# One block of the program instead of two in a retention, short-convolution and product-key expert step

## The reference, cut to what matters

```python
mod = silu(c) @ W_ada + b_ada            # 6 parts: shift, scale, gate, twice
h = rms_norm(x, g_pre1) * (1 + scale1) + shift1
q, k, v, g, bg, cg, xv = split(h @ W_in) # 7 groups of 512 columns
m = concat(retention(q, k, v, g), short_conv(bg, cg, xv)) @ W_out
x = x + gate1 * rms_norm(m, g_post1)
h = rms_norm(x, g_pre2) * (1 + scale2) + shift2
# experts: 128 * 128 of them, 8 heads, 16 chosen in each head
s = (h @ W_q) . sub_keys                 # 16 score sets of 128 a token
s1, s2 = top16 of each half; top16 of the 256 sums s1 + s2
f = sum over chosen e of softmax(top)[e] * gelu(h . u_tab[e]) * v_tab[e]
x = x + gate2 * rms_norm(f, g_post2)
```

## Time and profile before

| | |
|---|---|
| median of 3 runs | 1785.98 us (1785.57 to 1786.85) |
| the profiled execution | 1788.07 us, its span 1786.3 us |
| mean granted TensorE clock | 0.991 |
| TensorE busy | 1737.2 us, 97% of the span |
| VectorE, ScalarE, GpSimd busy | 1095.5, 587.0, 1052.1 us |

### The profile page before, as it was taken

The page is one execution under the profiler, slowest core; times in us unless marked ns, Lnnn a source line. Parts: engine busy times, 40 slices in busy tenths (PEclk is TensorE's granted clock), DMA queues, the critical chain, the costliest instruction groups (busy, mean ns, idle before and its releaser), DMA issues.

```text
span 1786.3 us, 31229 instructions
## 1 busy us (share of the span) xinstructions
PE 1737.2 (97%) x12724; PEld 1695.1 (95%) x12724; DVE 1095.5 (61%) x2204; ACT 587.0 (33%) x764; POOL 1052.1 (59%) x693
## 2 busy tenths in 40 slices
PE   7989999999999999999999999999999999999996
PEld 5989979699999999999999999999999999999996
DVE  5624586567477456667562222225888989888884
ACT  5222264332233323232222222223333333333332
POOL 0330100006687888888888888873667787767631
PEclk9999999999999999999999999999999999999997
DMA  8523399673466665666657666668999999999971
GB/s 327 189 83 120 122 363 322 216 233 83 99 130 134 139 126 125 143 126 126 143 119 146 139 142 142 132 138 313 363 354 358 362 364 370 367 366 376 380 295 48
DMA packets 192358, 385.18 MB, mean 216 GB/s; under 512 B 74376, under 2 KB 132104, under 8 KB 177368
## 3 DMA queue, kind: packets, MB, share of 16 engines
q1 hardware_dynamic: 111864, 306.56, 50.5%
q0 software_dynamic: 80352, 76.65, 19.7%
HBM read 318.44 MB, written 64.19 MB: 214 GB/s over the span
## 4 chain that ended last, share of the span: by engine, by line
PE 51%; DVE 10%; issue 7%; POOL 3%; DMA 2%; ACT 0%; DVEq 0%; SPq 0%; ACTq 0%
PE ps L1672 27%; PE ps L1692 23%; DVE ul L1862 2%; DMA qp<-vtab,packed_choice 2%; POOL qp L1826 2%; POOL ag L1819 1%; DVE topi L135 1%; DVE top L129 1%; DVE topi L125 0%; PE ps L1649 0%; DVE h L214 0%; DVE h L223 0%; DVE h L228 0%; DVE pick L218 0%; DVE pick L235 0%
## 5 line engine op out<-in xcount | busy, mean ns | idle before, releaser
L100 POOL DMA_INDIRECT gates_dram<-gate,where x384 | 646.6, 1684 | 271.0 <-DVE where L251 130.9
L1672 PE MATMUL ps<-hl,uh 128*128 128x260 f32 x2048 | 414.3, 283 | 7.6 <-DVE ul L1862 7.6
L1672 PE MATMUL ps<-hh,ul 128*128 128x260 f32 x2048 | 414.0, 284 | 0.0
L1672 PE MATMUL ps<-hh,uh 128*128 128x260 f32 x2048 | 413.4, 284 | 0.0
L1862 DVE TENSOR_TENSOR ul<-us,uh 128x1024 fp32r<-128x1024 f32 x132 | 161.0, 1223 | 365.0 <-issue 280.4
L1692 PE MATMUL ps<-cl,uh 128*128 128x384 f32 (+1 forms) x1024 | 345.2, 337 | 3.2 <-DVE ul L1862 1.8
L1692 PE MATMUL ps<-ch,ul 128*128 128x384 f32 x1024 | 344.1, 336 | 0.0
L1692 PE MATMUL ps<-ch,uh 128*128 128x384 f32 x1024 | 344.1, 336 | 0.0
L1672 PEld LDWEIGHTS ps<-hl,uh 128*128 128x128 f32 x2048 | 317.0, 189 | 8.8 <-DVE ul L1862 8.6
L1672 PEld LDWEIGHTS ps<-hh,ul 128*128 128x128 f32 x2048 | 317.0, 189 | 0.0
L1672 PEld LDWEIGHTS ps<-hh,uh 128*128 128x128 f32 x2048 | 316.2, 189 | 0.0
(11 more groups left out here) (245 smaller groups left out, 2240.6 us busy)
## 6 DMA issues: line engine op xcount, KB each, us to landing
us<-utab SPq DMA_DIRECT2D x128, 512.0 KB
pairs<-vtab SPq DMA_DIRECT2D x62, 1024.0 KB
gates_dram<-blank SPq DMA_DIRECT2D x24, 1024.0 KB, 9.7
ahead_dram<-a SPq DMA_DIRECT2D x128, 192.0 KB
qp<-ahead_dram SPq DMA_DIRECT2D x32, 768.0 KB
gt<-gates_dram SPq DMA_DIRECT2D x32, 768.0 KB
wr<-w_ada SPq DMA_DIRECT2D x21, 1024.0 KB, 7.7
wr<-w_in SPq DMA_DIRECT2D x13, 1024.0 KB, 4.8
```

The source lines that it names most:

```text
L100: nc.gpsimd.indirect_dma_start(out=io["gates"].rearrange("g p c a t -> (g p c a t)").unsqueeze(1), out_offset=bass.IndirectOffsetOnAxis(ap ...
L1672: last = nc.tensor.matmul(out[:, half, :], w, r[:, k, half * TH:(half + 1) * TH], start=(k == 0 and q == 0), stop=(k == KD - 1 and q == 2))
```

## The change

It has five parts.

1. **One block.** Both stages return their programs as functions, and one block runs them one after the other on each engine. There is no barrier between them. TensorE takes expert block 0 straight behind the last query block, and the scores of sets 12 to 15 (`scores(0, 3, 4)`) behind expert block 0 instead of ahead of it. ScalarE makes the high parts of the first two expert tiles (`first_weights`) behind query block 13 of 16.
2. **v.** The samples' chunk (bank 4) goes first; each chunk waits only for the reader of its own banks, and the copies are awaited apart (`vs_ok` ahead of block `G0`, `v_ok` ahead of the next).
3. **First norm.** VectorE adds the two squared slices of each pair, and TensorE sums four slices instead of eight.
4. **`between(9)`** in place of `between(8)` at the second place in `decide`, for all tiles but the first.
5. **Scatters.** None are in the mixer's part; `(0, 0)` leads the list, and the order of tile 1 and tile 2 is changed from the twelfth place on, so that `(1, 7)` stands between `(2, 5)` and `(2, 6)`.

```diff
-    between(8)
+    between(9 if i else 8)
     settle()
     nc.vector.tensor_tensor(gate.rearrange("p (h k) -> p h k", h=n), ex,
...
+            @block.tensor
+            def _(pe):
+                mixer["tensor"](pe)
+                peer["tensor"](pe)
+
+            @block.scalar
+            def _(act):
+                mixer["scalar"](act, peer["first_weights"])
+                peer["scalar"](act)
...
-                for k in range(KD):
-                    norm_sums(k, sq_ok, 1 + k // 2)
+            for n in range(KD // 2):
+                pe.wait_ge(added_ok, n + 1)
+                for a in range(2):
+                    last = nc.tensor.matmul(pair(SUMS)[:, a, :], ones, mix[:, 2 * n, a * TH:(a + 1) * TH],
+                                            start=(n == 0), stop=(n == KD // 2 - 1))
+            last.then_inc(ss_mm, 1)
...
-                all_read()
                 for half in range(2):
                     s = parts()
-                    for c in range(CHUNKS + 1):
+                for c in (CHUNKS, *range(CHUNKS)):
+                    if half == 0 and c % 2 == 0:
+                        pe.wait_ge(*read_of(V_BANKS.index(c) + made[0] - RING))
...
+                    if half and c == CHUNKS:
+                        last.then_inc(vs_mm, 1)
                     last.then_inc(v_mm, 1)
-                pe.wait_ge(v_ok, 2)
-                blocks(8)
+            def copied(m):
+                if m == G0:
+                    pe.wait_ge(vs_ok, 1)
+                elif m == G0 + 1:
+                    pe.wait_ge(v_ok, 1)
+            blocks(8, opened=copied)
...
+                    act.wait_ge(vs_mm, 1)
+                    nc.scalar.activation(vs[:], ps[:, CHUNKS, :], ACT.Copy).then_inc(vs_ok, 1)
                         act.wait_ge(v_mm, 2)
                         nc.scalar.activation(vt[:], ps[:, 0:CHUNKS, :], ACT.Copy).then_inc(v_ok, 1)
-                        nc.scalar.activation(vs[:], ps[:, CHUNKS, :], ACT.Copy).then_inc(v_ok, 1)
...
+            for n in range(KD // 2):
+                dve.wait_ge(sq_ok, n + 1)
+                nc.vector.tensor_tensor(mix[:, 2 * n], mix[:, 2 * n], mix[:, 2 * n + 1], ALU.add).then_inc(added_ok, 1)
                 inverse_rms(1)
...
-                scores(0, 3, 4)
                 for m in range(NK):
                     pe.wait_ge(ul_ok, m + 1)
-                    if m >= 3:
+                if m < 2:
+                    pe.wait_ge(io["qp_ok"], 2 * PH - 1 + m)
+                elif m == 2:
+                    pe.wait_ge(s_ok, 3)
+                else:
                         pe.wait_ge(a_ok, m - 2)
...
+        def first_weights(act):
+            act.wait_ge(io["wl_ok"], io["splits"])
+            for m in range(LEAD):
+                high(act, m)
```

More of the change, by code:

```diff
@@ new lines, in modulation_ahead @@
+            def modulation_ahead(k):
+                if k == 1:
+                    for _ in range(3):
+                        ada_product()
+                        ada_turn()
+                if k == 2:
+                    ada_turn()
+            blocks(4, lambda k: (first_hl, k + k // 2 + 2), together=True, ahead=modulation_ahead)
+            pe.wait_ge(mod_ok, PAIRS)
+            for half in range(2):
+                s = parts()
+                for c in (CHUNKS, *range(CHUNKS)):
+                    if half == 0 and c % 2 == 0:
+                        pe.wait_ge(*read_of(V_BANKS.index(c) + made[0] - RING))
+                    first = min(c * P, T - P)
+                    for k in range(KD):
+                        hi, lo = (r[:, k, first:first + P] for r in (hh, hl))
+                        for q, (w, r) in enumerate(((hi, s[1]), (hi, s[0]), (lo, s[0]))):
+                            last = nc.tensor.matmul(ps[:, c, half * WC:(half + 1) * WC], w, r[:, k, :],
+                                                    start=(k == 0 and q == 0), stop=(k == KD - 1 and q == 2))
+                    if half and c == CHUNKS:
+                        last.then_inc(vs_mm, 1)
+                last.then_inc(v_mm, 1)
@@ new lines, in tensor_program, with behind @@
+            ada_step()
+            variance_sums(RH - 1)
+            ada_turn()
+            def behind(b):
+                if b == 1:
+                    pe.wait_ge(st_ok, RH)
+                    pe.wait_ge(mod_ok, PAIRS + 1)
+            out_blocks(behind)
+            for at, (sem_of, count, k) in enumerate(((m_sum, KD - 2, 0), (m_ok, KD, KD - 1))):
+                pe.wait_ge(sem_of, count)
+                for a in range(2):
+                    last = nc.tensor.matmul(pair(SUMS)[:, a, :], ones, mix[:, k, a * TH:(a + 1) * TH],
+                                            start=(at == 0), stop=(at == 1))
@@ new lines, in tensor_program, with turn_within, scores_behind @@
+            last.then_inc(ss_mm, 1)
+            all_read()
+            ada_step(first=True)
+            ada_step()
+            pe.wait_ge(ms_ok, 2)
+            for k in range(KD):
+                norm_sums(k, sq_ok, KD // 2 + k + 1)
+            ada_step()
+            ada_step()
+            def turn_within(k):
+                if k == 4:
+                    ada_turn()
+            def scores_behind(b):
+                if b == 1:
+                    pe.wait_ge(mod_ok, PAIRS + 2)
+                for j in range(0 if b == 2 else b - 1, min(b, EARLY_SETS)) if b >= 2 else ():
+                    if j == 0:
+                        pe.wait_ge(io["in_keys"], 16)
+                    g = j // 4
+                    if j % 4 == 0 and g >= 2:
+                        pe.wait_ge(io["s_ok"], g - 1)
+                    pe.wait_ge(qp_ok, j + 1)
+                    last = nc.tensor.matmul(ps[0:TT, 6 + g % 2, (j % 4) * NK:(j % 4 + 1) * NK], qp[:, j, 0:TT],
+                                            io["keys"][:, j, :], start=True, stop=True)
+                    if j % 4 == 3:
+                        last.then_inc(io["s_mm"], 1)
```

2287 lines of the change are left out of this document (1118 added, 1169 removed).

## The result

The changed kernel took 1764.0 us, median of 4 runs (1763.1 to 1764.2), beside 1786.4 for the kernel before on the same chip: ratio 0.9871, 95% interval 0.9857 to 0.9884, 1.3% or some 23 us faster. A second set of 4 runs on another chip gave 1761.8 (1761.0 to 1762.8), ratio 0.9866 (0.9851 to 0.9880). The forecast was 1762.2, range 1759.5 to 1769.0.

A forecast was written before the change was run, and what follows sets the result against it. TensorE, busy 97% of the span, was taken to set the time, so gains come from its idle time or clock. Terms 6.4 + 5.2 + 2.4 + 9.8 = 23.8 us off 1785.98 gave 1762.2 us, range 1759.5 to 1769.

The forecast's parts named there:

- Border, 6.4: Border of the two blocks: one block gains 6.4 us, about 3 the wait and the rest mostly clock.
- v, 5.2: At v: the waits for VectorE's rotation (2.4) and ScalarE's copy (2.5) go, gaining 5.2 us.
- Tails, 9.8: Decisions' tails: `between(9)` removes the waits for `ul` and the slow clock behind them, gaining 9.8 us.
- The margins of 1.1 and 0.9 us: Last decision's tail: low parts ready with 1.1 and 0.9 us to spare; rival that they don't hold, 0.10, 1767.6 us.
- The 0.3 us put behind the two shorter waits: Tails: some 0.3 us of the gain counted behind the two waits other than the longest, beside its 1.7.
- First norm, 2.4: Start: summing pairs makes the sum some 2.5 us earlier; 0.1 taken off for a weight tile, gain 2.4 us.
- the first sum runs slow: Rival, 0.12: the first norm's rows stay at 0.4 us, part 3 gains only 1.0, total 1763.6 us.
- Scatters, "enough by 3.7 us": Before the second loop: SyncE waits 6.5 us for scatters, coefficients still 3.7 us early; cost 0, upper bound some 6.
- Sum: Whole kernel: 6.4 + 5.2 + 2.4 + 9.8 = 23.8 us gained, from the median 1785.98 to 1762.2 us.
- such a wait's going: Second loop: one more of TensorE's short waits may vanish, given as the reason for the range below the forecast.
- Slower, by the scatters: SyncE's wait for 384 scatters: a chain 27.5 us longer brings back all 23.8 us; chance of slower 0.02.

The follow-up runs named there:

- two_blocks: Changed kernel cut into two blocks of the program again, first 20 scatters ahead of the cut, new order inside each engine kept: 1768.5 us, 0.9901.
- v_old: Changed kernel with part 2 undone: v waits for all banks, samples' chunk last, the block behind v waits for both copies: 1768.5 us, 0.9910.
- warm: Changed kernel plus ten fp32 matmuls of 512 columns on constants at the start, into a bank nobody reads: 1767.0 us, 0.9881.
- best2: Changed kernel with fewer filler matmuls on constants at the start, and SyncE storing the next expert tile ahead of its first load of coefficients: 1761.8 us, 0.9865.
- scores_first: Changed kernel, still one block, with the last early scores ahead of expert block 0 again and the same move on ScalarE: 1764.4 us, 0.9867.
- before_tails: Kernel before with part 4 alone, one more low part in each decision behind tile 0's: 1776.1 us, 0.9949.
- norm_old: Changed kernel with part 3 undone: TensorE sums all eight slices of squares (32 rows), VectorE adds none: 1764.3 us, 0.9875.
- late_keep: Changed kernel with a GpSimd memset delaying the last scatters, and SyncE storing the next expert tile ahead of its first coefficient load: 1764.0 us, 0.9875.

## Why the prediction was right, and where it was not

- **Border, 6.4.** Measured 6.5, and two_blocks alone gives 6.1 back. Both halves, the wait and the low clock around it, are in the rows.
- **v, 5.2.** Measured 5.4, with both waits back in v_old. The trace of the kernel before had no low clock at these waits; in v_old the clock fell behind the first of them, and they cost 7.1.
- **Tails, 9.8.** Measured 9.5. The margins of 1.1 and 0.9 us in the last tail held, with 1.3 and 1.1. The 0.3 us put behind the two shorter waits aren't there: the clock stayed up behind them.
- **First norm, 2.4.** The step is right as a mean (2.5 over the traces, three of them with the old sum), and the term was off by 2.1 in the trace shown: the rival "the first sum runs slow" came true in it, 14 rows of 16 at 0.43 us, and a second piece of low clock followed, which no rival had. What I took for the pace of a stretch is one of several that the same program shows. The rows agree with the rule of the Trainium skill cited there (TensorE: Matmul & The Clock Gate, "What's actually happening"), that the clock starts low and activity releases it, as far as the slow rows at the start go; but keeping TensorE busier there (warm, best2) gained nothing that a run shows.
- **Scatters, "enough by 3.7 us".** This step failed. The end of the chain was forecast well: landed at 1189.1, issued 1188.59 (the chain started 1.8 us later than forecast, since the first norm gave less, and was 8.2 instead of 5.9 us shorter). Of the 8.2, 4.4 are the barrier's pause. The other 3.8 aren't the one landing that the forecast counted with 1.8: waits put down to landings fell from 18.6 to 14.1 us, but a new one of 4.7 without a releaser stands at 540.90, and the scatters' own time fell by 3.6. But I followed only the coefficients behind SyncE's wait, and only named the stores that stand there too. The spare of the stores is used up at 9 us ahead of block 127, which is where the changed kernel stands: 0 to 0.75 us lost in it and its near variants, 2.75 when the chain is 3.9 us longer. That so little was lost is luck: the forecast's own numbers put the load at 1189.1 and block 127 at 1219.1 - 23.8 = 1195.3, 6.2 us ahead, for which the table has a loss of some 2 us (an estimate between its rows at 8.1 and 5.6). scores_first, whose scatters are the changed kernel's, had such a longer chain by itself and lost 3.3.
- **Sum.** 21.2 us of the 24.0 lie ahead of the second loop, 2.6 less than forecast: 2.1 at the start, 0.3 in the tails and 0.4 at the stores, less 0.3 at v and the border. The 2.8 us behind it make the sum come out, and that is luck and not the mechanism: no edit stands there, the traces spread over 8 us there, and the profiled execution of the kernel before took 2.1 us more than its median, the changed one's 0.1. In the trace before, 1.8 of them are waits in the loop (1.75 and 0.52, now 0.43); the prediction had such a wait's going as its lower bound. What causes them isn't shown. The medians' difference, 22.4 and 24.1 us in the two sets, has the forecast's 23.8 between its values.
- **Slower, by the scatters.** The point from which it decides was put at 27.5 us; by the table it is nearer, some 24 us counted from the chain as measured. The mechanism is real (before_tails), its size was not reached. The scatters' own busy time changed little, 643.0 us now and 646.6 before (640.6 to 647.8 over all traces), so the contention that the Trainium skill (GPSIMD Engine Reference, "Key points") speaks of, if it is in these durations, stuck to VectorE's work, as it was counted.

What stays open: why the clock is low for 0, 3.4 or 6.8 us behind the same rows, and what makes a gathered row late in the second loop. No run took either apart. Part 5 wasn't tried by itself: no run has the old order of the scatters in one block.

## What to carry to other kernels

When TensorE's waits are removed one after the other, follow every queue that had slack beside it, and price all that is queued behind its wait, stores first: they need to land, behind whatever loads were issued ahead of them. A wait of 3 to 4 us of TensorE cost up to twice its length here (6.1 for the barrier, 5.6 for the longest tail), because the clock fell behind it. And before a term of one or two us is read out of a single trace, look at the same stretch in a second one of the same kernel.

## What the runs showed of the hardware

- At the start the page's clock column reads 1.00 while fp32 rows of 260 columns stand 0.43 us apart; later they stand 0.22 apart without any change of the code. In best2 the column reads 0.57 over rows at 0.43. So the column doesn't show the low pace at the very start; the distance of the rows does.
- TensorE's rows came to full pace 4.0 us (kernel before) and 6.2 us (changed kernel) behind the first one, without a pause in both, and 4.4 us in the second trace of the changed kernel.
- Which waits of TensorE were followed by a clock of 0.5 (3.4 or 6.8 us of it), behind the start and ahead of the last wait for VectorE: all eleven of 2.88 us or more (up to 5.71); of seven between 2.4 and 2.7 us two (v_old's 2.42 and norm_old's 2.70, while the kernel before had 2.41 and 2.46 without); of fourteen between 1.1 and 1.9 us one, 1.86 in late_keep, while another of 1.86, in the kernel before, had none.
- A store of one tile, issued behind two loads of 1.5 MB and two weight tiles on the same queue, was awaited 10.6 us, with the DMA engines' share at 1.00 (late_keep); one behind the first such load and one tile 7.0 us (changed kernel).
- Executions of the changed kernel and its variants differ by up to 3 us at the start and 8 us in the second loop; a median of 4 or 5 runs doesn't tell 1 us.
